# Rotary halves exchanged by small DMAs, and output squares added on VectorE, in a differential attention on one core

## The reference, cut to what matters

```python
def _apply_partial_rotary(x, cos, sin):        # ROT_DIM = 32, half = 16
    x1, x2 = xr[..., :half], xr[..., half:]    # xr: the first 32 of the 128 features
    rot = concatenate([x1 * cos - x2 * sin, x2 * cos + x1 * sin], axis=-1)
    return concatenate([rot, x[..., ROT_DIM:]], axis=-1)

q = _apply_partial_rotary(_rmsnorm(q, q_g), cos, sin)
k = _apply_partial_rotary(_rmsnorm(k, k_g), cos, sin)
sc = einsum('bqhcd,bkhcd->bhcqk', q, k) * scale          # masked, then softmax: p
w = p[:, :, 0] - lam * p[:, :, 1]
o = einsum('bhqk,bkhe->bqhe', w, v)
o = _rmsnorm(o, subln_g) * (1.0 - lambda_init)           # over the 256 features of a head
h = h + o.reshape(b, s, A_V_WIDTH) @ w_o
```

## Time and profile before

| what | us |
|---|---|
| median of 3 runs (lowest, highest) | 2820.35 (2820.33, 2820.63) |
| time of the profiled execution | 2819.36 |
| its span, first to last instruction | 2817.58 |
| TensorE busy in it | 2750.5 (98%) |
| VectorE busy | 1980.3 (70%) |
| ACT busy | 1190.4 (42%) |
| differential attention, all heads | from about 509 to 850 |

### The profile page before, as it was taken

The page is one execution under the profiler, slowest core; times in us unless marked ns, Lnnn a source line. Parts: engine busy times, 40 slices in busy tenths (PEclk is TensorE's granted clock), DMA queues, the critical chain, the costliest instruction groups (busy, mean ns, idle before and its releaser), DMA issues.

```text
span 2817.6 us, 44014 instructions
## 1 busy us (share of the span) xinstructions
PE 2750.5 (98%) x15284; PEld 2386.6 (85%) x15284; DVE 1980.3 (70%) x2609; ACT 1190.4 (42%) x1517; POOL 5.7 (0%) x12
## 2 busy tenths in 40 slices
PE   6999999999999999999999999999999999999999
PEld 5787888888878888888888888888888888888888
DVE  6555477676767777766777766688777775677765
ACT  1102454444444444444444443355444444444443
POOL 0000000000000000000000000000000000000000
PEclk9999999999999999999999999999999999999999
DMA  9886665544545666666666566654466666666664
GB/s 295 292 259 202 208 193 180 176 138 149 156 135 161 189 185 189 191 190 188 191 188 190 183 198 190 186 164 128 148 189 184 189 189 194 186 190 187 189 202 146
DMA packets 704736, 527.14 MB, mean 187 GB/s; under 512 B 31693, under 2 KB 694031, under 8 KB 704399
## 3 DMA queue, kind: packets, MB, share of 16 engines
q1 hardware_dynamic: 701728, 523.67, 61.7%
q10 hardware_dynamic: 2927, 2.39, 0.3%
HBM read 523.87 MB, written 2.10 MB: 187 GB/s over the span
## 4 chain that ended last, share of the span: by engine, by line
PE 89%; DVE 6%; issue 2%; ACT 2%; DMA 1%; ACTq 0%; SPq 0%; DVEq 0%
PE acc L649 75%; PE acc L729 2%; PE acc L717 2%; PE acc L918 2%; DVE wr L1656 1%; PE turned L729 1%; PE sums L729 1%; DVE pro_ada L1731 1%; PE sums L657 1%; PE mixed L839 1%; PE sums L1033 1%; DMA aring<-in_w_ada 1%; PE mixed L1038 0%; ACT wr L1215 0%; ACT three_L L1591 0%
## 5 line engine op out<-in xcount | busy, mean ns | idle before, releaser
L649 PE MATMUL acc<-xs,wr 128*128 128x512 f32 (+1 forms) x7680 | 1354.1, 337 | 1.5 <-DVE wr L1656 1.5
L649 PEld LDWEIGHTS acc<-xs,wr 128*128 128x128 f32 x7680 | 1174.4, 188 | 169.3 <-issue 7.2
L1656 DVE TENSOR_TENSOR wr<-raw,wr 128x1024 fp32r<-128x1024 f32 x832 | 1001.3, 1222 | 354.5 <-ACT wr L1215 340.6
L1215 ACT ACTIVATE wr<-raw 128x1024 fp32r<-128x1024 f32 x832 | 871.2, 1058 | 802.3 <-PE acc L649 792.1
L649 PE MATMUL acc<-ys,wr 128*128 128x512 f32 (+1 forms) x4352 | 764.5, 338 | 6.8 <-DVE ys L1690 6.6
L649 PEld LDWEIGHTS acc<-ys,wr 128*128 128x128 f32 x4352 | 667.9, 189 | 98.8 <-DVE ys L1690 6.4
L649 PE MATMUL acc<-wr,xs 128*128 128x512 f32 (+1 forms) x1024 | 189.0, 342 | 0.0
L649 PEld LDWEIGHTS acc<-wr,xs 128*128 128x128 f32 x1024 | 157.6, 188 | 26.6 <-issue 4.3
L1549 ACT ACTIVATE ffn_cv<-ffn_cv 128x256 f32<-128x256 f32 x88 | 36.9, 420 | 245.4 <-DVE ffn_cv L2230 245.4
L1667 DVE TENSOR_REDUCE ffn_ug<-acc 128x512 f32<-128x1024 f32 x88 | 107.8, 1225 | 39.5 <-PE acc L649 39.5
L1731 DVE SCALAR_TENSOR_TENSOR pro_ada<-aring,small,pro_ada 128x512 f32<-128x512 f32 (+1 forms) x112 | 92.4, 825 | 30.4 <-DMA aring<-in_w_ada 23.8
(11 more groups left out here) (306 smaller groups left out, 1531.4 us busy)
## 6 DMA issues: line engine op xcount, KB each, us to landing
raw<-in_ffn_w_up SPq DMA_DIRECT2D x704, 256.0 KB
raw<-in_ffn_w_down SPq DMA_DIRECT2D x160, 512.0 KB
raw<-in_a_w_qkv SPq DMA_DIRECT2D x96, 512.0 KB
raw<-in_b_w_kv SPq DMA_DIRECT2D x64, 512.0 KB
aring<-in_w_ada SPq DMA_DIRECT2D x96, 256.0 KB, 6.5
w<-in_w_in SPq DMA_DIRECT2D x48, 512.0 KB
raw<-in_w_ada SPq DMA_DIRECT2D x32, 512.0 KB, 6.1
raw<-in_w_out SPq DMA_DIRECT2D x32, 512.0 KB
```

Source lines behind the costliest of these rows:

```text
L649: mm = pe.matmul(*ops, start=first and ops is wide, stop=last and ops is wide)
L1215: f(wr[:, s, :, 0:256], raw[:, s, :].rearrange("p (k n) -> p k n", k=UK), ACT.Copy)\
L1656: tt(wr[:, s, :, 256:512], raw[:, s, :].rearrange("p (k n) -> p k n", k=UK), wr[:, s, :, 0:256], ALU.subtract).then_inc(T.unit_split[s].se ...
```

## The change

- The constants lose the block `C_TURN_A`. The column of rotary frequencies for this attention gets a sign: minus for the first 16 of each 32 partitions, plus for the other 16. So the sine table has the sign that the matrix had (cosine doesn't feel it).
- TensorE's `diff_turn` goes, for q and for k. In its place ACT issues two DMAs each (`turn_copy`): 16 partitions of q (2 KB each) to the other half's partitions of a new tile `qturn`, and the other way round; the same for k into `kturn`. `turn_copy(qturn, qA)` stands behind the weight copies ahead of k's squares, `turn_copy(kturn, kA)` behind the output's squares, ahead of `hi(2)`. VectorE's rotary steps read `qturn` and `kturn` and wait for 32 on the new semaphore `turn_in`.
- The scores wait for all four marks of `heads_out` of a head, where the second and third were waited for by `diff_turn` before.
- Of the two sums of the output's squares one stays: VectorE adds the squares of both halves into one 128x256 tile, and TensorE waits for that (`out_squares`) in place of ACT's squares. In `diff_out` VectorE does one split between the signal to ACT and this add, and one fewer behind the low half. The last head has no split there.

```diff
+    out[:, C_COLS * P + 1] = np.tile(np.concatenate([-inv2, inv2]), P // ROT)
...
             def diff_scores(c):
                 if c == 0:
-                    pe.wait_ge(*T.heads_out.next())
+                    pe.wait_ge(*T.heads_out.next(4))
...
-            def diff_turn(src, k):
-                pe.wait_ge(*T.heads_out.next(1 + k))
-                pe.wait_ge(*T.mixed_read.next())
-                pe.matmul(mixed[:, :], const(C_TURN_A), flat(src[:, :, :]), start=True, stop=True)\
-                    .then_inc(T.mixed_ready.sem, 1)
...
             def diff_out_sums():
-                pe.wait_ge(*T.sq_ready.next())
+                T.sq_ready.n += 1
+                pe.wait_ge(*T.out_squares.next())
                 sums_bank()
-                feature_sums(sq[0], ones[:, :], sums[:, 0:TOK]).then_inc(T.sums_ready.sem, 1)
+                pe.matmul(sums[:, 0:TOK], ones[:, :], sq[0][:, 0, :], start=True, stop=True).then_inc(T.sums_ready.sem, 1)
...
+            def turn_copy(to, x, done):
+                act.wait_ge(*T.heads_out.next(done))
+                for a, b in ((0, ROT // 2), (ROT // 2, 0)):
+                    act.dma_start(to[a:a + ROT // 2, :, :], x[b:b + ROT // 2, :, :]).then_inc(T.turn_in.sem, 16)
...
                     hi(2)
+                    turn_copy(qturn, qA, 1)
                     act.wait_ge(*T.acc_read.next())
                     squares_of(S[1], 1)
                     hi(1)
                     root(2 * TOK, HD)
                     if live:
                         diff_out_squares()
+                    turn_copy(kturn, kA, 2)
+                    T.heads_out.n += 1
                     hi(2)
...
+            def head_turn(x, turned_x):
+                here, m = x[0:ROT, :, :], tmp[1][0:ROT, :, :]
+                dve.wait_ge(*T.turn_in.next(32))
+                tt(m, turned_x[0:ROT, :, :], both(sinA)[0:ROT, :, :], ALU.mult)
+                step(tt(here, here, both(cosA)[0:ROT, :, :], ALU.mult))
+                own()
+                tt(here, here, m, ALU.add).then_inc(*T.heads_out.one())
...
                 dve.tensor_copy(small[:, 47:48], oA[:, 0, 0:1]).then_inc(*T.for_act.one())
+                if turn:
+                    split_units(1)
+                dve.wait_ge(*T.sq_ready.next(3 if turn else 1))
+                tt(sq[0][:, 0, :], sq[0][:, 0, :], sq[0][:, 1, :], ALU.add).then_inc(*T.out_squares.one())
                 dve.wait_ge(*T.rs_ready.next())
...
-                    split_units(2)
+                    split_units(1 if live else 2)
                     evac(vA[:, :, :], by="partitions")
```

More of the change, by code:

```diff
@@ L118 @@
 PACK_ROWS = [P, _at - P, P, P, VEC_END - 4 * P]
-C_IDENT, C_ONES64, C_TURN, C_TURN_A, C_TRI, C_CAUSAL, C_CHUNK, C_CAP, C_STRICT, C_COLS = range(10)
+C_IDENT, C_ONES64, C_TURN, C_TRI, C_CAUSAL, C_CHUNK, C_CAP, C_STRICT, C_COLS = range(9)
 def constants():
-    out = np.zeros((P, 9 * P + 2), np.float32)
+    out = np.zeros((P, C_COLS * P + 2), np.float32)
     block = lambda n: out[:, n * P:(n + 1) * P]
@@ L133, in constants @@
     block(C_TURN)[:] = same * ((k % ROPE == m % ROPE - half) * 1.0 - (k % ROPE == m % ROPE + half))
-    half = ROT // 2
-    small = (k < ROT) & (m < ROT)
-    block(C_TURN_A)[:] = small * ((k == m - half) * 1.0 - (k == m + half))
     block(C_TRI)[:] = k >= m
@@ L145, in constants @@
     inv2 = np.power(np.float32(500000.0), f, dtype=np.float32)
-    out[:, 9 * P] = np.tile(inv1, P // len(inv1))
-    out[:, 9 * P + 1] = np.tile(inv2, P // len(inv2))
+    out[:, C_COLS * P] = np.tile(inv1, P // len(inv1))
+    out[:, C_COLS * P + 1] = np.tile(np.concatenate([-inv2, inv2]), P // ROT)
     return out
@@ L182 @@
     "for_act", "for_dve", "res_ready", "c_in", "cols_ready",
-    "squares_summed", "gate_used", "gate_summed", "dve_step", "act_step", "store0", "store1"]
+    "squares_summed", "turn_in", "out_squares", "gate_used", "gate_summed", "dve_step", "act_step", "store0", "store1"]
 class Tallies:
@@ L198, in __init__ @@
          self.table_ready, self.for_act, self.for_dve, self.res_ready, self.c_in, self.cols_ready,
-         self.squares_summed, self.gate_used, self.gate_summed,
+         self.squares_summed, self.turn_in, self.out_squares, self.gate_used, self.gate_summed,
          self.dve_step, self.act_step, self.store0, self.store1, *slots) = [Tally(s) for s in sems]
@@ L209, in __init__ @@
                     self.table_ready, self.for_act, self.for_dve, self.res_ready, self.c_in,
-                    self.cols_ready, self.squares_summed,
+                    self.cols_ready, self.squares_summed, self.turn_in, self.out_squares,
                     self.gate_used, self.gate_summed, self.dve_step, self.act_step, self.store0, self.store1, *slots]
@@ L315, in program @@
         raw = sb("raw", [RING, UK * 256])
-        cst = sb("cst", [9 * P + 2])
+        cst = sb("cst", [C_COLS * P + 2])
         ones = sb("ones", [P])
@@ L383, in program @@
         oA = o("o", [2, TOK])
+        qturn, kturn = o("qturn", [2, TOK]), o("kturn", [2, TOK])
         o = Overlay("three_", tail)
@@ L1069, in in_k @@
                             tokens_roots(1)
-                        if n == 3:
-                            diff_turn(qA, 0)
                     def in_v(n):
@@ L1079, in in_v @@
                             diff_out_sums()
-                        if n == 3:
-                            diff_turn(kA, 1)
                     pair(lambda k: xs[:, k, :], before=None if live else normed, after=in_q)
@@ L1088, in _ @@
             with T.turns(pe, A_HEADS // 2 - 1, **splits(24), acc_read=6, heads_out=8, scores_read=4, sq_ready=6,
-                         sums_read=6, mixed_read=6, weights_ready=2, turned_read=2):
+                         sums_read=6, mixed_read=2, weights_ready=2, turned_read=2, out_squares=2):
                 two_heads(False)
@@ L1526, in _ @@
             with T.turns(act, A_HEADS // 2 - 1, unit_used=24, acc_read=6, max_ready=4, scores_ready=4, scores_read=4,
-                         sums_ready=6, sums_read=6, turned_ready=2, turned_read=2, for_act=2, split_me=2,
+                         sums_ready=6, sums_read=6, turned_ready=2, turned_read=2, for_act=2, split_me=2, heads_out=8,
                          raw_in0=6 * UNIT, raw_in1=6 * UNIT, raw_in2=6 * UNIT, raw_in3=6 * UNIT) as i:
@@ L1784, in _ @@
             for e in range(2):
-                w = ts(ang[:, e, :], S[1][:, e, :], cst[:, 9 * P + e:9 * P + e + 1], None, ALU.mult)
+                w = ts(ang[:, e, :], S[1][:, e, :], cst[:, C_COLS * P + e:C_COLS * P + e + 1], None, ALU.mult)
             step(w)
@@ L2190, in two_heads @@
                     split_units(1)
-                    head_turn(qA)
+                    head_turn(qA, qturn)
                     head_norm(kA, S[1], "a_k_norm_g_2")
@@ L2194, in two_heads @@
                     if live:
-                        diff_out(slice(0, 2) if first else bass.ds(i * 4 + (2 + 2 * e), 2), lambda: head_turn(kA))
+                        diff_out(slice(0, 2) if first else bass.ds(i * 4 + (2 + 2 * e), 2), lambda: head_turn(kA, kturn))
                     else:
-                        head_turn(kA)
-                    split_units(2)
+                        T.sq_ready.n += 2
+                        head_turn(kA, kturn)
+                    split_units(1 if live else 2)
                     evac(vA[:, :, :], by="partitions")
@@ L2202, in _ @@
             with T.turns(dve, A_HEADS // 2 - 1, unit_used=24, hi_ready=24, acc_read=6, scores_ready=4, max_ready=4, scores_read=4,
-                         weights_ready=2, rs_ready=6, heads_out=8, mixed_ready=6, mixed_read=6, for_act=2, split_me=2,
-                         hi_out=2, lo_out=2, dve_step=20) as i:
+                         weights_ready=2, rs_ready=6, heads_out=8, mixed_ready=2, mixed_read=2, for_act=2, split_me=2,
+                         hi_out=2, lo_out=2, dve_step=20, turn_in=128, sq_ready=6, out_squares=2) as i:
                 two_heads(False, i)
@@ L2211, in _ @@
             diff_out(slice(14, 16))
-            T.sq_ready.n += 3 * A_HEADS
             residual_product(gain=VEC["ffn_norm_g_2"], first_splits=3)
```

## The result

| what | before | after |
|---|---|---|
| median of 20 runs each (lowest, highest), us | 2820.01 (2813.46, 2820.86) | 2823.74 (2817.41, 2826.85) |
| span of the profiled execution, us | 2817.6 | 2822.7 |
| TensorE busy in it, us | 2750.5 | 2742.0 |

The ratio is 1.0016, with a 95% interval of 1.0009 to 1.0023: a little slower, 4 to 5 us, clear of zero, and by its middle inside the 0.2% that the prediction called no change. The forecast was 2805, with a range of 2800 to 2818. So some 19 us are to be explained, and they came back inside the one stage that was changed.

The account below looks back on a forecast made before the run. TensorE, busy 98% of the span, was taken to bound the kernel. Removed work of 17.3 us and old waits of 4.7, less 7.0 of new wait, gave -15.0 us: 2805.3 from 2820.35, with a range of 2800 to 2818.

Parts of the forecast that it names:

- Its removals: TensorE in the differential attention: 13.8 us of rotary products and 3.4 us of output-square sums go, together 17.3 us.
- the waits for the split and most of those for the exponentials: TensorE's old waits, 1.5 us for a VectorE weight split and 3.2 for ACT's exponentials: both taken as gone, 4.7 us.
- 22.0 us would go: Differential attention: 17.3 us of removed TensorE work and 4.7 us of old waits, before any new wait is counted.
- Its path to the sums: Per head: k's norm, ACT's squares, k's two DMA issues, ACT's weight copy, moved split, add; sums ready at 573.05, wanted 572.07.
- its reading that ACT issues a DMA beside the running activation: ACT's queue: a DMA issue, 0.39 us, starts with the activation ahead of it, so q's issues cost ACT nothing.
- rival B: ACT issues a DMA only when the activation ahead has ended: wait 2.2 us a head, net -6.6, 2813.8 us; 22%.
- q's exchange: in time or not: q's DMAs land 2.1 to 2.5 us after issue, at 564.1 to 564.5; VectorE wants them at 564.65: in time, by little.
- a new wait of 1.0 us: TensorE at the sums of the output squares waits for VectorE's add: 1.0 us in seven heads, 7.0 us in all.
- the lower bound of the wait: TensorE's wait at the sums if k's DMA issues on ACT's queue are hidden wholly: 0.7 us a head.
- The rule of the Trainium skill: q's exchange, held to the end of the weight burst: an estimated 0.3 us late, 2.1 us worse over seven heads.
- Rival D: No change in time: q's exchange lands late, after 4.0 to 5.6 us, giving 2815 to 2826 us; 9%.
- Rival A: The new wait at the sums is absent, so 22.0 us go: 2798.3 us; 7%.

Follow-up runs that it names:

- q_early: The changed kernel, but ACT issues q's exchange one weight copy sooner: 2809.20 us, ratio 0.9967.
- k_later: On top of q_early, k's exchange is issued behind the next weight copy instead of ahead of it: 2800.53 us, ratio 0.9936.
- squares_only: The kernel before, with only the VectorE add of the output squares and its moved split, without the exchange by DMAs: 2814.98 us, ratio 0.9989.
- wait_7: Changed kernel with q's exchange one weight copy sooner and split behind add, plus seven dummy VectorE additions ahead of the add in seven heads: 2827.77 us.
- wait_4: Changed kernel with q's exchange one weight copy sooner and split behind add, plus four dummy VectorE additions ahead of the add in seven heads: 2801.27 us.

## Why the prediction was wrong

It was wrong by its size of one wait and by a cost that it left out: 9.9 us more wait in the seven heads and 8.6 us of lower clock, beside 1.0 of old waits that stayed and 0.5 in the last head (which the prediction called even, though its 17.3 counts that head's 0.43 as gained). Its removals held: 48 records, the waits for the split and most of those for the exponentials (its 4.7 us were 3.7), and "22.0 us would go" is what the runs without the new wait show, 22 to 25 us. Its path to the sums held step by step, and so did its reading that ACT issues a DMA beside the running activation (646.36 against 646.28 to 647.34); rival B falls.

The step that failed is "q's exchange: in time or not", and with it "a new wait of 1.0 us". Measured in the seven heads it was 16.9 us, 2.4 a head:
- q's exchange: an issue takes 0.61 us in the median and not 0.39, and the landing 3.2 and not 2.1 to 2.5. That median is of both DMAs; the second, for which VectorE waits, took about 3.0 to 4.0, an estimate from the start of the pair, 0.55 us for the first issue, and the end of VectorE's wait in heads 2 to 8. So it is not in time by 0.1 to 0.5 us but late by 0.4 to 1.6. From after to q_early TensorE's wait falls by 6.2 us, 0.9 a head.
- k's issues: 0.56 us each, and ACT's copy starts 0.8 us later than before (1.36 against 0.54 behind the squares' start) where 0.3 was put. From q_early to k_later: 5.7 us, 0.8 a head.
- the moved split with the copy that it waits for: what is left in k_later (5.0 us, 0.7 a head) and the whole of squares_only (0.8 a head). This was 0.7 in the prediction, the lower bound of the wait.

The lines of the changed kernel's DMA view (size of each DMA, median us to landing) and the issues' own durations in ns:

```profile
two_qturn<-two_q ACTq DMA_DIRECT2D x16, 32.0 KB, 3.2
two_kturn<-two_k ACTq DMA_DIRECT2D x16, 32.0 KB, 2.8
...
L1478 ACTq DMA_DIRECT2D two_qturn<-two_q x16: 514/612/1315, 522.7 to 821.0; - x16
L1478 ACTq DMA_DIRECT2D two_kturn<-two_k x16: 514/562/669, 530.1 to 830.4; - x16
```

The rows taken for the landing were 1.7 and 2.1, both with idle DMA engines; the median of the stores, most of them amid weight loads, was 3.7. The prediction knew of the burst of weights at that time and still took the idle rows. DMA share and GB/s behind the issue in the head above (the second q DMA is issued at about 647, and VectorE's step that waits for it starts at 650.96):

```profile
647.00:648.00 1.00, 1.00 (x7) 0.89 (x6) 0.97 (x2) 0.34 (x1) 0.00 (x0) 1.00 0.85 227
648.00:649.00 1.00, 1.00 (x6) 0.64 (x5) 0.88 (x2) 0.63 (x1) 0.00 (x0) 1.00 0.98 323
649.00:650.00 1.00, 1.00 (x4) 0.50 (x4) 0.58 (x1) 0.91 (x1) 0.00 (x0) 1.00 0.11 38
```

It lands one to two us after the bulk of the burst is over. k's exchange is issued beside a burst too and takes 2.8; what makes the difference between the two is open. The rule of the Trainium skill that the prediction weighed ("DMA: Bandwidth & Descriptors", section on queues, rings and completion order: a DMA's semaphore is written after the earlier writes of its engine) pointed the right way, with a larger price than the 0.3 us put on it; no run here shows that this is the mechanism, and plain sharing of the engines would give the same sign. The same page's section "Issuing engines are not separate DMA queues" calls the issuing time usually small beside the DMA: here an issue of k's took 0.56 us beside 2.8 to its landing, a fifth, and on this path the pair was worth 0.8 us a head.

The cost left out is the clock, 8.6 us. Without it the change would have been at about 2815, inside the range. The prediction called no price for a wait but its length, and wait_7 shows that it has another. Rival D's time was right (2815 to 2826), but by luck: it wanted landings of 4.0 to 5.6 us for what came from 3.2 and the clock. Rival A, no new wait at all, is what the split behind the add makes true.

## What to carry to other kernels

When work moves off the engine that bounds, write down the path to the result that it will wait for, and put nothing on it that can stand behind: here one weight split ahead of a 0.42 us add turned a gain of 22 us into a loss of 4. Take the duration of a small DMA from rows with the traffic that it will meet, and its issue as time of the queue that issues it. Two changes that each gain may share a path; run each alone before the pair.

## What was not expected of the hardware

- At the sums, a wait of TensorE of 2.6 us or more was followed by half the clock every time (11 of 11 in two kernels), at 1.5 to 1.7 us each, beyond the wait; up to 1.6 us never (28 of 28 in the seven heads of q_early, k_later, squares_only and wait_4; the last head, where waits follow each other closely, is not counted). In between, with two waits at the scores, 1.85 and 1.86 us were followed by it and 1.82, 1.85 and 2.19 were not.
- An exchange between partitions, two DMAs of 16 partitions and 32 KB each, takes 1.16 us of ACT's queue and, by the medians of the runs, 2.7 to 3.8 us from the issue of one to its landing; issued earlier (q_early), q's took longer to land (3.7 for 3.2), so that moving a DMA ahead by 2.8 us did not bring it 2.8 us sooner.
